# Three down-projections of a two-block layer: every second slab's remainder by ScalarE and an adding transfer

## The chip, the cores and the metric

The program runs on one core of a Trainium2 chip. A core has five engines that work beside each other, each with its own queue of instructions, and they meet through semaphores: TensorE (PE) multiplies, VectorE (DVE) and ScalarE (ACT) work element by element, GpSimd (POOL) does so too and its queue also issues transfers, and SyncE (SP) here only issues transfers. Sixteen DMA engines carry out the transfers of all queues. The metric is the time of one execution in device microseconds. A number like L487 is a line of the kernel before.

## The reference, cut to what matters

Two residual blocks work on 256 tokens of width 2048, in float32. The first has three attention branches, the second a pooling and a convolution branch and, at its end, a feed-forward part of width 8192. The change touches only that last part:

```
u = rms_norm(h, g_pre_mlp)
f = jnp.square(jax.nn.relu(u @ w_up)) @ w_down      # w_up 2048 x 8192, w_down 8192 x 2048
h = h + rms_norm(f, g_post_mlp)
```

## The kernel before

**Products in three passes.** TensorE multiplies in the rounded type fp32r. To keep the precision of float32 each weight w is split into `high`, w rounded to fp32r, and a remainder `low = w - high`; the left operand x is split in the same way. Each product then runs as x_high * high, x_high * low and x_low * high into the same bank (L607 to L609).

**Slabs.** All weights of the program form one stream of slabs of 512 KB. A slab of a down-projection is two blocks of 128 rows by 512 columns, and takes 12 matmuls on TensorE (two blocks, two tiles of tokens, three passes). Four stations handle each slab n:
1. SP loads it into `stage_rows`, which has STAGES = 8 slots, when slab n-8 has been split (`load_slab`, L464).
2. ScalarE rounds it into `high_rows`, which has PAIRS = 4 slots, as `low_rows` has, when TensorE is done with slab n-4 (`round_high`, L476). The count of finished slabs is the semaphore `used`.
3. VectorE writes the remainder into `low_rows` (`subtract_low`, L487) and raises `split_done`.
4. TensorE waits for `split_done` and multiplies (`multiply`).

**Order.** Each engine's order is fixed in the program. ScalarE and VectorE split the slab that is four ahead of the one just finished, and between slabs they do the other work of the stage (`stream`). The feed-forward part runs in four quarters of the hidden width: `w_up0` to `w_up3`, each followed by its `w_down0` to `w_down3`. A `w_down` job has 4 steps of 512 output columns with 8 slabs each, so 32 slabs. Its left operand `f_pair` was made in the `w_up` job before it. After each step VectorE adds the two banks of results to `y_rows`. In this stage ScalarE has nothing but the rounding.

**The POOL queue** issues a few transfers over the whole program: the bias rows for the gates (L757), the table `toep` (L720), a second copy of x (L772), and two gain vectors, each spread to 128 partitions, well ahead of the feed-forward part (L795, L796). In the last job it scales six pieces of the output (L802).

Of the kernel before, what the change touches and what calls it, by code (L numbers as in the profile page):

```python
# [23 lines left out]
F32R = mybir.dt.float32r  # L24
# [141 lines left out]
def build(nc, A, out):  # L166
    ctx = ExitStack()
    with ctx:
# [127 lines left out]
        def s(name):  # L296
            if name not in S:
                S[name] = sem(name)
            return S[name]
# [152 lines left out]
        stream_of_slabs = [(job, step, idx) for _, job in order for step in range(job.steps) for idx in range(job.S)]  # L452


        def load_slab(sp, job, i, u, idx):
            step = i * job.unroll + u
            n, n_static = job.slab(i, u, idx)
            p, _, k, kt, _ = job.pieces[idx]
            slot = n_static % STAGES
            sp.wait_ge(split_done, n + 1)  # L460
            sp.sem_inc(issued, 1)
            rows = slice((p.row0 + k) * P, (p.row0 + k + kt) * P)
            src = p.w[rows, bass.ds(p.col0 + step * p.stride, p.cols)] if p.stride else p.w[POOL_ORDER[step], :, :]
            sp.dma_start((stage_rows if p.by_rows else stage)[:, slot, 0:kt, 0:p.cols], src.rearrange("(k p) n -> p k n", p=P)).then_inc(landed[slot], 16)  # L464

        def round_high(act, job, i, u, idx):
            n, n_static = job.slab(i, u, idx)
            p, _, k, kt, _ = job.pieces[idx]
            slot, pr = n_static % STAGES, n_static % PAIRS
            act.wait_ge(landed[slot], 16 * (n_static // STAGES + 1) + i * (16 * (job.unroll * job.S // STAGES)))  # L470
            if job is jobs["w_up_first"] and idx < 3:
                act.activation(first_high[:, idx], stage_rows[:, slot], ACT.Copy).then_inc(high_done, 1)
                return
            act.wait_ge(used, n + 1)
            src, high = (stage_rows, high_rows) if p.by_rows else (stage, w_high)
            act.activation(high[:, pr, 0:kt, 0:p.cols], src[:, slot, 0:kt, 0:p.cols], ACT.Copy).then_inc(high_done, 1)  # L476

        def subtract_low(dve, job, i, u, idx):
            n, n_static = job.slab(i, u, idx)
            p, _, k, kt, _ = job.pieces[idx]  # L480
            slot, pr = n_static % STAGES, n_static % PAIRS
            dve.wait_ge(high_done, n + 1)
            if job is jobs["w_up_first"] and idx < 3:
                dve.tensor_tensor(first_low[:, idx], stage_rows[:, slot], first_high[:, idx].bitcast(F32), ALU.subtract).then_inc(split_done, 1)
                return
            src, high, low = (stage_rows, high_rows, low_rows) if p.by_rows else (stage, w_high, w_low)
            dve.tensor_tensor(low[:, pr, 0:kt, 0:p.cols], src[:, slot, 0:kt, 0:p.cols],  # L487
                              high[:, pr, 0:kt, 0:p.cols].bitcast(F32), ALU.subtract).then_inc(split_done, 1)
# [89 lines left out]
        def multiply(pe, job, i, u, beside=None, between=None, first_slab=None):  # L578
            for idx, (p, part, k0, kt, last) in enumerate(job.pieces):
# [16 lines left out]
                    pe.wait_ge(s(name), before + ((0 if p.stride else 2 * u) + k0 + kt + 1) // 2)  # L596
                if not by_k:
                    pe.wait_ge(split_done, STAGES + n + 1)
                for k in range(kt if p.rows else 0):
                    if by_k:  # L600
                        by_k(idx, k)
                    first, final = k0 + k == 0, last and k == kt - 1
                    high, low = (v[:, pr, k, 0:p.cols] for v in ((high_rows, low_rows) if p.by_rows else (w_high, w_low)))
                    for t in range(2):
                        bk = acc[:, 2 * bank + t, 0:p.cols]
                        x_high, x_low = (p.rows[:, k0 + k, half, t * P:(t + 1) * P] for half in range(2))
                        pe.matmul(bk, x_high, high, start=first, stop=False)  # L607
                        pe.matmul(bk, x_high, low, start=False, stop=False)  # L608
                        mm = pe.matmul(bk, x_low, high, start=False, stop=final)  # L609
# [43 lines left out]
        def _(sp):  # L653

            def other_params():
                sp.dma_start(params[:, N0:PARAMS], A["params"][:, N0:PARAMS]).then_inc(s("params_in"), 16)
                sp.dma_start(relT[:], A["rel_bias_t"]).then_inc(s("params_in"), 16)
                sp.dma_start(sinks, A["sinks_b"].partition_broadcast(P)).then_inc(s("sinks_in"), 16)

            x_of_rows = A["x"][0] if A["x"].shape[0] == 1 else A["x"]  # L660
            for name in names:
                job = jobs[name]
                if name == "mem_kv":
# [19 lines left out]
                            other_params()  # L683
                    sp.wait_ge(s("pair_ready"), 8)
                    sp.dma_start(mem_in[:], A["mem"].rearrange("(t p) d -> p t d", p=P)).then_inc(s("mem_rows_in"), 16)
                    continue
                repeat(sp, job.steps, job.unroll, lambda i, u: [load_slab(sp, job, i, u, idx) for idx in range(job.S)])
            for e in range(8):
# [7 lines left out]
        def _(pool):  # L696
# [70 lines left out]
                load_bias(n)  # L767

            pool.wait_ge(s("pv_copied"), len(HEADS))
            pool.dma_start(meta_in[:], A["meta_2"]).then_inc(s("meta_in"), 16)  # L770
            pool.dma_start(meta_t[:], A["meta_t"]).then_inc(s("meta_in"), 16)
            pool.dma_start(x_rows[:], (A["x"][0] if A["x"].shape[0] == 1 else A["x"]).rearrange("(t p) d -> p t d", p=P)).then_inc(s("x_back"), 16)  # L772
            gated(5, late[:, L_BQ:L_BQ + 6, :], L_BGATE, 6)
            for n in (10, 11):
                load_bias(n)
# [16 lines left out]
                    reach *= 2  # L792
                pool.sem_inc(s("windowed"), 1)
            pool.wait_ge(used, PAIRS + jobs["conv_out"].slab0)
            pool.dma_start(mix_gain[:], A["g_post_mix_2"].partition_broadcast(P)).then_inc(s("mix_gain_in"), 16)  # L795
            pool.dma_start(gain_rows[:], A["g_post_mlp_2"].partition_broadcast(P)).then_inc(s("gain_in"), 16)  # L796
            pool.wait_ge(s("gain_in"), 16)
            for e in range(6):
                r, t = e // 2, e % 2
                v = y_rows[:, t, r * ROW:(r + 1) * ROW]  # L800
# [5 lines left out]
        def _(act):  # L806
# [72 lines left out]
            def beside_mem(n):  # L879
                if n == 6:  # L880
                    act.wait_ge(s("x_in"), 64)
                    row_squares(x_in, "x", 0, "input_squared")
                if n == 7:
                    act.wait_ge(s("input_squared"), 1)
                    row_squares(x_in, "x", 1, "input_squared")
                    chain_root(0)
                if n == 10:
                    act.wait_ge(s("params_in"), 32)
                if n == 14:
                    mem_evacuate(0, mk_rows)  # L890
                if 11 <= n < 15:
                    for q in (2 * (n - 11), 2 * (n - 11) + 1):
                        high_unit(hT, "norm_g", q, 8)
                if n == 15:
                    mem_evacuate(1, mv_rows)
# [220 lines left out]
            def beside_up_b(n):  # L1116
                silu("w_up_b", 5, 16, L_BGATE, 3, n)
                merged_high("w_up_b", n)
                if n == 34:
                    act.wait_ge(s("meta_in"), 32)  # L1120
                    act.wait_ge(s("sums_set"), 1)
                    for r in range(4):
                        if r >= 1:
                            act.wait_ge(s("meta_squared"), r)
                        act.activation(rstd[0:META, 0:ROW], meta_in[:, r * ROW:(r + 1) * ROW], ACT.Square,
                                       accum_out=sums_1[0:META, 2, r:r + 1]).then_inc(s("meta_squared"), 1)
# [216 lines left out]
        def _(pe):  # L1343
# [332 lines left out]
            products("w_up_first", lambda n: turn_h2(3) if n == 4 else None, turn_rest)  # L1676
            for q in range(4):
                products(f"w_up{q}", turn_f if q == 0 else None)
                products(f"w_down{q}", (lambda n: None) if q == 3 else None)


        @block.vector
        def _(dve):
# [105 lines left out]
            def beside_mem(n):  # L1789
# [4 lines left out]
                    for t in range(2):  # L1794
                        dve.tensor_scalar(x_in[:, t, :], x_in[:, t, :], rs_col("x", t), None, ALU.mult).then_inc(s("x_scaled"), 1)
                if n == 9:
                    dve.wait_ge(s("params_in"), 32)
                    for i, (a, b) in enumerate((("q_norm_a", "k_norm_a"), ("q_norm_c", "k_norm_c"), ("q_norm_b", "k_norm_b"))):
                        link(dve.tensor_tensor(k_gain[:, i:i + 1], column(a), column(b), ALU.mult))
                if n == 12:  # L1800
# [47 lines left out]
            def head_logits(h):  # L1848
# [24 lines left out]
                dve.wait_ge(dve_link, link.n)  # L1873
                if kind == "B":
                    if c == 0:
                        dve.wait_ge(s("sinks_in"), 16)
                    link(dve.tensor_scalar(negmax[:, b, :], negmax[:, b, :], sinks[:, c:c + 1], -1.0, ALU.max, ALU.mult))
                elif kind == "C":
                    by_token = rs[:, RS["cq"] + c:RS["cq"] + c + C_HEADS + 1:C_HEADS]
# [220 lines left out]
            def wo_body(i, u, part):  # L2100
# [1 line left out]
                r = 2 * i + u  # L2102
                cols = slice(r * ROW, (r + 1) * ROW)
                if r == 0:
                    dve.wait_ge(s("x_back"), 16)
                for t in range(2):
                    dve.tensor_tensor(h_rows[:, t, cols], banks[:, t, :], x_rows[:, t, cols], ALU.add).then_inc(s("h1_rows"), 1)
                dve.wait_ge(s("h1_rows"), 2 * r + 2)
# [8 lines left out]
            def beside_wo(n):  # L2117
                merged_low("w_o", n)
                if n == META_AT + 1:
                    dve.wait_ge(s("meta_in"), 32)  # L2120
                    dve.wait_ge(s("merged_ready"), 8)
                    dve.wait_ge(s("meta_squared"), 4)
                    g0 = COL["g_pre_mix_2"]
# [205 lines left out]
            def mixed_body(i, u, part):  # L2329
# [2 lines left out]
                    return  # L2332
                banks, _ = group_done(dve, jobs["w_o_2"], i, u)
                if r == 0:
                    dve.wait_ge(s("mix_gain_in"), 16)
                for t in range(2):
                    dve.wait_ge(s("mix_squared"), 2 * r + t + 1)
                    gained(banks, r, t)
# [109 lines left out]

            def last_down():

                dve.wait_ge(s("gain_in"), 16)
                dve.wait_ge(s("row_squared"), 6)
                link(dve.tensor_reduce(out_rest, row_sums[:, :, 0:3], AX, ALU.add))
                link(dve.scalar_tensor_tensor(out=out_rest, in0=out_rest, scalar=1.0 / D, in1=eps_3, op0=ALU.mult, op1=ALU.add))
# [70 lines left out]
```

## Time and profile before

| | |
|---|---|
| two runs | 2048.28 and 2049.4 us, median 2048.84 us |
| span of the profiled execution | 2046.3 us |
| its own time | not listed apart from the two runs; they lie 2.0 to 3.1 us above the span |
| TensorE busy | 2034.2 us, 99% |
| VectorE, ScalarE, GpSimd busy | 66%, 46%, 4% |
| granted TensorE clock, mean | 0.999 of full speed |
| DMA | 389.23 MB, mean 190 GB/s |

The span runs from the first to the last instruction. Busy time says how long an engine had work under way, not whether somebody waited for it. The ends of matmuls are modelled, and a matmul of 512 columns is shown with 0.39 us although the next one starts 0.227 us after it; the time of a slab is therefore read from the starts. A transfer's time to landing runs from its issue to the moment at which its semaphore is complete.

### The profile page before, as it was taken

Reading aid. Unit: us, or ns where it says so; the run is one execution under the profiler, and the core shown is the slowest. Engines: PE = TensorE matmul, PEld = TensorE weight load, DVE = VectorE, ACT = ScalarE, POOL = GpSimd, SP = SyncE. Lnnn points to the kernel's source line nnn. Section 1 sums busy time; section 2 is a strip of 40 time slices with the busy share of each in tenths; the row PEclk is TensorE's granted clock in tenths of the full one; section 3 lists DMA queues with packets and bytes.
Section 4 is the critical chain, followed back from the end, with each engine's and each line's share of the span. In section 5 each row is a group of like instructions: output and inputs, shape, how many; then the busy total and the mean of one; then the engine's idle time right before and its main releaser. Section 6 shows DMA issues by size and latency. Waiting matters only on the chain.

```text
span 2046.3 us, 29256 instructions
## 1 busy us (share of the span) xinstructions
PE 2034.2 (99%) x10572; PEld 1732.4 (85%) x10572; DVE 1358.7 (66%) x1815; ACT 948.2 (46%) x1225; POOL 80.7 (4%) x91
## 2 busy tenths in 40 slices
PE   9999999999999999999999999999999999999998
PEld 7888898888888888999888888888888888888886
DVE  6766756576756565678999756576556556645655
ACT  6645444565544444433444644553333333333343
POOL 0000102001011000002000000000000000000001
PEclk9999999999999999999999999999999999999999
DMA  9687555555566555555666565655565565555652
GB/s 348 196 199 189 176 155 182 183 168 180 185 217 220 192 188 187 171 175 158 193 194 200 181 232 185 196 171 189 194 189 185 194 195 181 196 191 184 194 195 103
DMA packets 265468, 389.23 MB, mean 190 GB/s; under 512 B 12504, under 2 KB 147032, under 8 KB 264571
## 3 DMA queue, kind: packets, MB, share of 16 engines
q1 hardware_dynamic: 262587, 377.19, 57.7%
q0 software_dynamic: 2624, 10.54, 2.0%
q8 instruction: 69, 1.13, 0.2%
q14 instruction: 44, 0.36, 0.1%
q10 hardware_dynamic: 144, 0.01, 0.0%
HBM read 385.02 MB, written 2.54 MB: 189 GB/s over the span
## 4 chain that ended last, share of the span: by engine, by line
PE 98%; SPq 1%; DMA 1%; DVE 0%; ACT 0%; issue 0%; DVEq 0%
PE acc L607 19%; PE acc L609 19%; PE acc L608 19%; PE acc L630 18%; PE acc L628 10%; PE acc L622 2%; PE acc L620 2%; PE acc L621 2%; PE acc L626 1%; PE aux L1489 1%; PE aux L1573 1%; DMA stage_rows<-in_w_mem_kv 1%; PE aux L1503 0%; PE acc L546 0%; PE acc L545 0%; PE acc L544 0%
## 5 line engine op out<-in xcount | busy, mean ns | idle before, releaser
L487 DVE TENSOR_TENSOR low_rows<-stage_rows,high_rows 128x1024 fp32r<-128x1024 f32 x438 | 540.2, 1237 | 404.1 <-ACT high_rows L476 399.2
L476 ACT ACTIVATE high_rows<-stage_rows 128x1024 fp32r<-128x1024 f32 x438 | 462.3, 1059 | 581.7 <-PE acc L609 531.0
L487 DVE TENSOR_TENSOR w_low<-stage,w_high 128x1024 fp32r<-128x1024 f32 (+1 forms) x264 | 320.7, 1221 | 230.8 <-ACT w_high L476 226.3
L476 ACT ACTIVATE w_high<-stage 128x1024 fp32r<-128x1024 f32 (+1 forms) x264 | 276.2, 1047 | 417.0 <-PE acc L630 298.9
L630 PE MATMUL acc<-u,w_high 128*128 128x512 f32 x900 | 247.9, 394 | 0.0
L607 PE MATMUL acc<-high_rows,f_pair 128*128 128x512 f32 x496 | 193.0, 389 | 0.0
L608 PE MATMUL acc<-low_rows,f_pair 128*128 128x512 f32 x496 | 192.9, 389 | 0.0
L609 PE MATMUL acc<-high_rows,f_pair 128*128 128x512 f32 x496 | 192.9, 389 | 0.0
L630 PE MATMUL acc<-hT,w_high 128*128 128x512 f32 x645 | 177.5, 394 | 0.0
L630 PEld LDWEIGHTS acc<-u,w_high 128*128 128x128 f32 x900 | 152.9, 189 | 19.0
L628 PEld LDWEIGHTS acc<-u,w_low 128*128 128x128 f32 x960 | 146.8, 188 | 20.6
L628 PE MATMUL acc<-u,w_low 128*128 128x256 f32 x960 | 152.5, 281 | 0.0
L607 PE MATMUL acc<-high_rows,hT 128*128 128x512 f32 x384 | 151.8, 395 | 0.0
L609 PE MATMUL acc<-high_rows,hT 128*128 128x512 f32 x384 | 149.6, 390 | 0.0
L608 PE MATMUL acc<-low_rows,hT 128*128 128x512 f32 x384 | 149.6, 390 | 0.0
L630 PEld LDWEIGHTS acc<-hT,w_high 128*128 128x128 f32 x645 | 109.6, 189 | 13.4
L628 PEld LDWEIGHTS acc<-hT,w_low 128*128 128x128 f32 x688 | 104.0, 189 | 15.6 <-issue 2.7
L628 PE MATMUL acc<-hT,w_low 128*128 128x256 f32 x688 | 112.0, 285 | 0.0
L620 PE MATMUL acc<-uT,w_high 128*128 128x272 f32 x384 | 111.1, 289 | 0.0
L622 PE MATMUL acc<-uT,w_high 128*128 128x272 f32 x384 | 110.8, 288 | 0.0
L621 PE MATMUL acc<-uT,w_low 128*128 128x272 f32 x384 | 110.4, 288 | 0.0
L608 PEld LDWEIGHTS acc<-low_rows,f_pair 128*128 128x128 f32 x496 | 93.1, 188 | 19.4
(409 smaller groups left out, 3348.0 us busy)
## 6 DMA issues: line engine op xcount, KB each, us to landing
stage_rows<-in_w_in SPq DMA_DIRECT2D x160, 512.0 KB, 3.6
stage<-in_w_in SPq DMA_DIRECT2D x136, 512.0 KB, 3.5
stage_rows<-in_w_down SPq DMA_DIRECT2D x128, 512.0 KB, 4.3
stage<-in_w_up SPq DMA_DIRECT2D x120, 512.0 KB, 3.9
stage_rows<-in_w_o SPq DMA_DIRECT2D x64, 512.0 KB, 3.6
stage_rows<-in_w_pool_out SPq DMA_DIRECT2D x16, 512.0 KB, 3.8
stage_rows<-in_w_conv_out SPq DMA_DIRECT2D x16, 512.0 KB, 4.5
stage_rows<-in_w_mem_kv SPq DMA_DIRECT2D x14, 512.0 KB, 11.6
```

The lines of the kernel that those rows point to most:

```text
L476: act.activation(high[:, pr, 0:kt, 0:p.cols], src[:, slot, 0:kt, 0:p.cols], ACT.Copy).then_inc(high_done, 1)
L487: dve.tensor_tensor(low[:, pr, 0:kt, 0:p.cols], src[:, slot, 0:kt, 0:p.cols], high[:, pr, 0:kt, 0:p.cols].bitcast(F32), ALU.subtract).then ...
L607: pe.matmul(bk, x_high, high, start=first, stop=False)
L608: pe.matmul(bk, x_high, low, start=False, stop=False)
L609: mm = pe.matmul(bk, x_low, high, start=False, stop=final)
L620: pe.matmul(dst, tile(w_high, k), b, start=first, stop=False)
L621: pe.matmul(dst, tile(w_low, k), a, start=False, stop=False)
L622: mm = pe.matmul(dst, tile(w_high, k), a, start=False, stop=final)
L626: pe.matmul(bk, tile(w_high, 0), p.rhs(0)[0], start=True, stop=False, skip_group_check=True)
L628: pe.matmul(bk[:, 0:T], tile(w_low, k), p.rhs(k0 + k)[1], start=False, stop=False, skip_group_check=True)
L630: mm = pe.matmul(bk, tile(w_high, k), p.rhs(k0 + k)[0], start=False, stop=last and k == kt - 1, skip_group_check=True)
L1489: mm = pe.matmul(aux[:, logits_bank(h), lo:hi], q[:, t * P:(t + 1) * P], k[:, 0:hi - lo], start=True, stop=True)
```

## The change

In `w_down0`, `w_down1` and `w_down2`, in the first three of the four steps, the slabs with an odd index (1, 3, 5, 7) get their remainder in another way. That is 3 x 3 x 4 = 36 slabs of the 128 of the down-projections.
- ScalarE rounds such a slab as before, and then writes the slab once more, rounded and negated, into its slot of `low_rows`. Negated and rounded it is -high.
- GpSimd's queue then issues a transfer that reads the same weights from device memory again and adds them to that slot: w + (-high) = low. Two semaphores in turn, `low_added0` and `low_added1`, say that it has landed.
- VectorE leaves the subtraction out. It waits for the one before and raises `split_done`.
- TensorE waits, ahead of an added slab, for its transfer too. SP waits for the transfer of slab n-8 before it loads slab n into the same slot of `stage_rows`, which ScalarE has read by then.
- SP's and TensorE's loops over these jobs are written out step by step.
- Waits are merged: the sinks count with the parameters, the two meta transfers with the second copy of x, and the two gains with each other.

```diff
@@ -452,12 +452,27 @@
         stream_of_slabs = [(job, step, idx) for _, job in order for step in range(job.steps) for idx in range(job.S)]
 
 
+        ADDED = {}
+        for q in range(3):
+            job = jobs[f"w_down{q}"]
+            for step in range(job.steps - 1):
+                for idx in range(1, job.S, 2):
+                    ADDED[job.slab0 + step * job.S + idx] = len(ADDED)
+        low_added = [sem(f"low_added{b}") for b in range(2)]
+
+        def wait_added(eng, n):
+
+            e = ADDED.get(n) if isinstance(n, int) else None
+            if e is not None:
+                eng.wait_ge(low_added[e % 2], 16 * (e // 2 + 1))
+
         def load_slab(sp, job, i, u, idx):
             step = i * job.unroll + u
             n, n_static = job.slab(i, u, idx)
             p, _, k, kt, _ = job.pieces[idx]
             slot = n_static % STAGES
             sp.wait_ge(split_done, n + 1)
+            wait_added(sp, n - STAGES if isinstance(n, int) else None)
             sp.sem_inc(issued, 1)
             rows = slice((p.row0 + k) * P, (p.row0 + k + kt) * P)
             src = p.w[rows, bass.ds(p.col0 + step * p.stride, p.cols)] if p.stride else p.w[POOL_ORDER[step], :, :]
@@ -474,6 +489,8 @@
             act.wait_ge(used, n + 1)
             src, high = (stage_rows, high_rows) if p.by_rows else (stage, w_high)
             act.activation(high[:, pr, 0:kt, 0:p.cols], src[:, slot, 0:kt, 0:p.cols], ACT.Copy).then_inc(high_done, 1)
+            if isinstance(n, int) and n in ADDED:
+                act.activation(low_rows[:, pr], stage_rows[:, slot], ACT.Copy, scale=-1.0).then_inc(s("low_negated"), 1)
 
         def subtract_low(dve, job, i, u, idx):
             n, n_static = job.slab(i, u, idx)
@@ -482,6 +499,10 @@
             dve.wait_ge(high_done, n + 1)
             if job is jobs["w_up_first"] and idx < 3:
                 dve.tensor_tensor(first_low[:, idx], stage_rows[:, slot], first_high[:, idx].bitcast(F32), ALU.subtract).then_inc(split_done, 1)
+                return
+            if isinstance(n, int) and n in ADDED:
+                dve.wait_ge(split_done, STAGES + n)
+                dve.sem_inc(split_done, 1)
                 return
             src, high, low = (stage_rows, high_rows, low_rows) if p.by_rows else (stage, w_high, w_low)
             dve.tensor_tensor(low[:, pr, 0:kt, 0:p.cols], src[:, slot, 0:kt, 0:p.cols],
@@ -596,6 +617,7 @@
                     pe.wait_ge(s(name), before + ((0 if p.stride else 2 * u) + k0 + kt + 1) // 2)
                 if not by_k:
                     pe.wait_ge(split_done, STAGES + n + 1)
+                    wait_added(pe, n)
                 for k in range(kt if p.rows else 0):
                     if by_k:
                         by_k(idx, k)
-                sp.dma_start(sinks, A["sinks_b"].partition_broadcast(P)).then_inc(s("sinks_in"), 16)
+                sp.dma_start(sinks, A["sinks_b"].partition_broadcast(P)).then_inc(s("params_in"), 16)
 
...
@@ -684,6 +706,11 @@
                     sp.wait_ge(s("pair_ready"), 8)
                     sp.dma_start(mem_in[:], A["mem"].rearrange("(t p) d -> p t d", p=P)).then_inc(s("mem_rows_in"), 16)
                     continue
+                if name in ("w_down0", "w_down1", "w_down2"):
+                    for step in range(job.steps):
+                        for idx in range(job.S):
+                            load_slab(sp, job, step // job.unroll, step % job.unroll, idx)
+                    continue
                 repeat(sp, job.steps, job.unroll, lambda i, u: [load_slab(sp, job, i, u, idx) for idx in range(job.S)])
             for e in range(8):
                 t, r = e // 4, e % 4
@@ -767,9 +794,9 @@
                 load_bias(n)
 
             pool.wait_ge(s("pv_copied"), len(HEADS))
-            pool.dma_start(meta_in[:], A["meta_2"]).then_inc(s("meta_in"), 16)
-            pool.dma_start(meta_t[:], A["meta_t"]).then_inc(s("meta_in"), 16)
-            pool.dma_start(x_rows[:], (A["x"][0] if A["x"].shape[0] == 1 else A["x"]).rearrange("(t p) d -> p t d", p=P)).then_inc(s("x_back"), 16)
+            pool.dma_start(meta_in[:], A["meta_2"]).then_inc(s("rows_back"), 16)
+            pool.dma_start(meta_t[:], A["meta_t"]).then_inc(s("rows_back"), 16)
+            pool.dma_start(x_rows[:], (A["x"][0] if A["x"].shape[0] == 1 else A["x"]).rearrange("(t p) d -> p t d", p=P)).then_inc(s("rows_back"), 16)
             gated(5, late[:, L_BQ:L_BQ + 6, :], L_BGATE, 6)
             for n in (10, 11):
                 load_bias(n)
@@ -792,9 +819,15 @@
                     reach *= 2
                 pool.sem_inc(s("windowed"), 1)
             pool.wait_ge(used, PAIRS + jobs["conv_out"].slab0)
-            pool.dma_start(mix_gain[:], A["g_post_mix_2"].partition_broadcast(P)).then_inc(s("mix_gain_in"), 16)
-            pool.dma_start(gain_rows[:], A["g_post_mlp_2"].partition_broadcast(P)).then_inc(s("gain_in"), 16)
-            pool.wait_ge(s("gain_in"), 16)
+            pool.dma_start(mix_gain[:], A["g_post_mix_2"].partition_broadcast(P)).then_inc(s("gains_in"), 16)
+            pool.dma_start(gain_rows[:], A["g_post_mlp_2"].partition_broadcast(P)).then_inc(s("gains_in"), 16)
+            pool.wait_ge(s("gains_in"), 32)
+            for n, e in ADDED.items():
+                job, step, idx = stream_of_slabs[n]
+                p, _, k, kt, _ = job.pieces[idx]
+                rows = p.w[(p.row0 + k) * P:(p.row0 + k + kt) * P, step * ROW:(step + 1) * ROW]
+                pool.wait_ge(s("low_negated"), e + 1)
+                pool.dma_start(low_rows[:, n % PAIRS], rows.rearrange("(k p) n -> p k n", p=P).bitcast(F32R), accum_op=ALU.add).then_inc(low_added[e % 2], 16)
             for e in range(6):
@@ -1676,7 +1709,7 @@
             products("w_up_first", lambda n: turn_h2(3) if n == 4 else None, turn_rest)
             for q in range(4):
                 products(f"w_up{q}", turn_f if q == 0 else None)
-                products(f"w_down{q}", (lambda n: None) if q == 3 else None)
+                products(f"w_down{q}", lambda n: None)
 
 
         @block.vector
```

The remaining hunks only put the merged semaphores into the waits: `params_in` at 48, `rows_back` at 48, `gains_in` at 32.

ScalarE's order, from the last slab of `w_up0` to slab index 3 of `w_down0`; `w_high` and `high_rows` are the rounded slabs, `landed` says that a load is there. Before:

```order
L476 ACTIVATE w_high<-stage 128x1024 [waits used,landed2]
L476 ACTIVATE high_rows<-stage_rows 128x1024 [waits used,landed3]
L476 ACTIVATE high_rows<-stage_rows 128x1024 [waits used,landed4]
L476 ACTIVATE high_rows<-stage_rows 128x1024 [waits used,landed5]
L476 ACTIVATE high_rows<-stage_rows 128x1024 [waits used,landed6]
L476 ACTIVATE high_rows<-stage_rows 128x1024 [waits used,landed7]
```

and with the change:

```order
L491 ACTIVATE w_high<-stage 128x1024 [waits used,landed2]
L491 ACTIVATE high_rows<-stage_rows 128x1024 [waits used,landed3]
L491 ACTIVATE high_rows<-stage_rows 128x1024 [waits used,landed4]
L493 ACTIVATE low_rows<-stage_rows 128x1024
L491 ACTIVATE high_rows<-stage_rows 128x1024 [waits used,landed5]
L491 ACTIVATE high_rows<-stage_rows 128x1024 [waits used,landed6]
L493 ACTIVATE low_rows<-stage_rows 128x1024
L491 ACTIVATE high_rows<-stage_rows 128x1024 [waits used,landed7]
```

After the rounding of every odd slab stands the negated one, and the roundings of later slabs are queued behind it.

SP's queue at the start of `w_down0`, before, where the loop's registers stand between the loads:

```order
L117 ISA
L464 ISA [waits split_done]
L464 DMA stage_rows<-in_w_down 128x2x512
L460 REGISTER_ALU
L464 ISA [waits split_done]
L464 DMA stage_rows<-in_w_down 128x2x512
```

and with the change:

```order
L117 COMPARE_AND_BRANCH
L479 DMA stage_rows<-in_w_down 128x2x512 [waits split_done] x9
L479 DMA stage_rows<-in_w_down 128x2x512 [waits split_done,low_added0]
L479 DMA stage_rows<-in_w_down 128x2x512 [waits split_done]
L479 DMA stage_rows<-in_w_down 128x2x512 [waits split_done,low_added1]
L479 DMA stage_rows<-in_w_down 128x2x512 [waits split_done]
```

The first nine loads wait as before. From then on every second load also waits for an adding transfer, and the loads behind it wait with it.

## Rows read from the trace of the kernel before

**Rows 1.** The page, part 1: busy us, share, instructions of each engine.
```profile
PE 2034.2 (99%) x10572; PEld 1732.4 (85%) x10572; DVE 1358.7 (66%) x1815; ACT 948.2 (46%) x1225; POOL 80.7 (4%) x91
```
**Rows 2.** Windows of the first and third down-projection: busy us and instructions of each engine.
```profile
core 0: us, PE busy (x) PEld busy (x) DVE busy (x) ACT busy (x) POOL busy (x), PEclk, DMA share, GB/s
1421.00:1508.00 87.00, 87.00 (x386) 72.02 (x385) 45.62 (x42) 33.93 (x32) 0.00 (x0) 1.00 0.59 193
...
1770.00:1857.00 87.00, 87.00 (x391) 72.24 (x390) 45.65 (x43) 33.72 (x33) 0.00 (x0) 1.00 0.58 193
```
**Rows 3.** Waits of TensorE's weight loads, 1340 to 2041 us: us, times, longest.
```profile
PEld aux L1573 <- DVE tmp L2405: 0.5, 1, 0.5
```
**Rows 4.** Timeline of weight loads, first down-projection: start us, us, engine, line, operation.
```profile
1439.70 0.19 PEld L607 LDWEIGHTS acc<-high_rows,f_pair 128*128 128x128 f32 x1
...
1447.86 0.19 PEld L607 LDWEIGHTS acc<-high_rows,f_pair 128*128 128x128 f32 x1
```
**Rows 5.** Timeline of ScalarE, there and one pair before.
```profile
1346.44 2.02 ACT L476 ACTIVATE w_high<-stage 128x1024 fp32r<-128x1024 f32 x2
...
1440.19 1.06 ACT L476 ACTIVATE high_rows<-stage_rows 128x1024 fp32r<-128x1024 f32 x1 [1.66 <-PE acc L609]
1442.91 1.06 ACT L476 ACTIVATE high_rows<-stage_rows 128x1024 fp32r<-128x1024 f32 x1 [1.66 <-PE acc L609]
```
**Rows 6.** Timeline of VectorE, same place.
```profile
1441.28 1.23 DVE L487 TENSOR_TENSOR low_rows<-stage_rows,high_rows 128x1024 fp32r<-128x1024 f32 x1 [1.49 <-ACT high_rows L476]
1444.00 1.23 DVE L487 TENSOR_TENSOR low_rows<-stage_rows,high_rows 128x1024 fp32r<-128x1024 f32 x1 [1.50 <-ACT high_rows L476]
```
**Rows 7.** DMA issues of all: queue, count, KB each, median us to landing.
```profile
stage_rows<-in_w_down SPq DMA_DIRECT2D x128, 512.0 KB, 4.3
...
stage_rows<-in_w_mem_kv SPq DMA_DIRECT2D x14, 512.0 KB, 11.6
...
bias_ring<-in_gate_bias POOLq DMA_DIRECT2D x12, 256.0 KB, 4.0
toep<-bias_rows POOLq DMA_DIRECT2D x8, 288.0 KB, 9.1
...
x_rows<-in_x POOLq DMA_DIRECT2D x1, 2048.0 KB, 11.8
...
mix_gain<-in_g_post_mix POOLq DMA_DIRECT2D x1, 1024.0 KB, 7.7
gain_rows<-in_g_post_mlp POOLq DMA_DIRECT2D x1, 1024.0 KB, 10.3
...
small<-in_sinks_b SPq DMA_DIRECT2D x1, 6.0 KB, 10.8
```
**Rows 8.** The POOL queue's issues at line 757: ns min/median/max.
```profile
L757 POOL DMA_DIRECT2D bias_ring<-in_gate_bias x12: 538/538/572, 351.4 to 661.2; - x12
```
**Rows 9.** Windows: the start, and a 2 MB transfer of the POOL queue.
```profile
0.00:100.00 100.00, 95.86 (x494) 80.42 (x495) 67.57 (x117) 64.30 (x107) 1.72 (x11) 1.00 0.82 275
14.00:32.00 18.00, 18.00 (x81) 14.89 (x80) 11.74 (x18) 10.49 (x17) 0.00 (x0) 1.00 1.05 386
606.00:616.00 10.00, 10.00 (x46) 8.28 (x45) 7.83 (x8) 4.52 (x6) 5.39 (x3) 1.00 0.99 353
```
**Rows 10.** Timeline of the POOL queue: two issues.
```profile
604.81 0.72 POOL L772 DMA_DIRECT2D x_rows<-in_x  x1
...
1193.84 0.55 POOL L796 DMA_DIRECT2D gain_rows<-in_g_post_mlp  x1
```
**Rows 11.** Sources of four lines: ns min/median/max, first and last start us.
```profile
L658 SPq DMA_DIRECT2D small<-in_sinks_b x1: 552/552/552, 21.1 to 21.1; - x1
L1799 DVE TENSOR_TENSOR k_gain<-params x3: 151/160/160, 44.2 to 44.6; 128x1 f32<-128x1 f32 x3
L1125 ACT ACTIVATE rstd<-meta_in x4: 615/630/632, 703.8 to 706.0; 16x512 f32<-16x512 f32 x4
L2327 DVE TENSOR_TENSOR mixed<-acc,mix_gain x8: 681/684/685, 1264.2 to 1332.2; 128x512 f32<-128x512 f32 x8
```

More of the change, by code:

```diff
@@ L887, in beside_mem @@
                 if n == 10:
-                    act.wait_ge(s("params_in"), 32)
+                    act.wait_ge(s("params_in"), 48)
                 if n == 14:
@@ L1119, in beside_up_b @@
                 if n == 34:
-                    act.wait_ge(s("meta_in"), 32)
+                    act.wait_ge(s("rows_back"), 48)
                     act.wait_ge(s("sums_set"), 1)
@@ L1796, in beside_mem @@
                 if n == 9:
-                    dve.wait_ge(s("params_in"), 32)
+                    dve.wait_ge(s("params_in"), 48)
                     for i, (a, b) in enumerate((("q_norm_a", "k_norm_a"), ("q_norm_c", "k_norm_c"), ("q_norm_b", "k_norm_b"))):
@@ L1875, in head_logits @@
                     if c == 0:
-                        dve.wait_ge(s("sinks_in"), 16)
+                        dve.wait_ge(s("params_in"), 48)
                     link(dve.tensor_scalar(negmax[:, b, :], negmax[:, b, :], sinks[:, c:c + 1], -1.0, ALU.max, ALU.mult))
@@ L2104, in wo_body @@
                 if r == 0:
-                    dve.wait_ge(s("x_back"), 16)
+                    dve.wait_ge(s("rows_back"), 48)
                 for t in range(2):
@@ L2119, in beside_wo @@
                 if n == META_AT + 1:
-                    dve.wait_ge(s("meta_in"), 32)
+                    dve.wait_ge(s("rows_back"), 48)
                     dve.wait_ge(s("merged_ready"), 8)
@@ L2334, in mixed_body @@
                 if r == 0:
-                    dve.wait_ge(s("mix_gain_in"), 16)
+                    dve.wait_ge(s("gains_in"), 32)
                 for t in range(2):
@@ L2449, in last_down @@
             def last_down():
-                dve.wait_ge(s("gain_in"), 16)
+                dve.wait_ge(s("gains_in"), 32)
                 dve.wait_ge(s("row_squared"), 6)
```

## Prediction, made before the changed kernel was run

> **What bounds the kernel now.** I read the busy time by engine first: TensorE is busy 2034.2 of 2046.3 us and VectorE 66% [rows 1]. The reader is to see that VectorE, which the change relieves, has a third of its time free. Next the windows of the down-projections that the change touches, of which the first and the third stand in the rows: in each 87 us TensorE is busy for all 87.00, VectorE for 45.6, ScalarE for 33.7 to 33.9, and the DMA engines have a share of 0.58 to 0.59 at 193 GB/s [rows 2]. Then the waits of TensorE's weight loads from 1340 us to the end: one, of 0.5 us, in another place [rows 3]. So TensorE never waits for VectorE in these stages, and taking work off VectorE can give back nothing there. Even if every idle microsecond of TensorE in the whole span went away, the gain would be 2046.3 - 2034.2 = 12 us, or 0.6%.
>
> What is left to work out is whether the new way gets its remainder to TensorE in time. The timeline gives the deadline. TensorE loads the first weights of a slab at 1439.70 and of the third after it at 1447.86 [rows 4]: 8.16 us for three slabs, 2.72 us for one. The rounding of slab n starts when slab n-4 is done, at 1440.19 [rows 5], and TensorE takes up slab n with that load at 1447.86.
>
> **The change part by part.**
>
> *VectorE* loses 36 subtractions of 1.23 us [rows 6], 44 us that nobody waited for: worth 0. Its order stays. At an added slab it only waits for the subtraction before, long over, and counts the slab as split.
>
> *ScalarE* gains 36 negated roundings. Two roundings of this size back to back take 2.02 us [rows 5], so the second ends at 1440.19 + 2.02 = 1442.21. The next rounding is due at 1442.91 [rows 5], so ScalarE keeps 0.7 us spare, and its queue costs 0.
>
> *The adding transfer* is the term that decides. VectorE starts 0.03 us after ScalarE's end (1440.19 + 1.06 = 1441.25, start 1441.28 [rows 5, 6]); with such a step the POOL queue issues at about 1442.25. From there to 1447.86 are **5.6 us** in which 512 KB must be issued, read, added and landed. Before the change the remainder was ready at 1442.51 and had 5.3 us to spare; this cover is used up entirely. No transfer of the kernel adds, so its landing time L is bounded by the nearest rows. All times to landing of this queue contain its own issue of 0.54 to 0.72 us [rows 8, 10].
> - From below: plain transfers of the POOL queue land in 4.0 us at 256 KB and 7.7 us at 1024 KB [rows 7]; between them 512 KB would take 4.0 + 3.7 x 256/768 = 5.2 us. That is just in time, with stall 0.
> - The middle: an adding transfer reads 512 KB from device memory and the same 512 KB of the destination, so 1024 KB go in. The row of that size says 7.7 us.
> - From above: 288 KB in short rows of 1 KB, a count of pieces (288) close to the 256 of this transfer, take 9.1 us. Plain 512 KB transfers in full queues, at the start, take 11.6 us [rows 7].
>
> I take 7.7 us, the row with the same bytes read and with ordinary loads beside it. It comes d = 7.7 - 5.6 = 2.1 us late.
>
> How stalls add up: slab n is late by d if the three slabs ahead of it ran without a wait. A stall at n-2, which is also an added slab, moves the start of n later, but not the moment at which its own preparation began, so it counts towards n. With s(n) + s(n-2) = d for neighbours, whatever the split, 12 added slabs of a job cost 6d, and the three jobs **18d = 18 x 2.1 = 38 us**. The last eight slabs of each job, and the fourth job, go the old way.
>
> A page of the Trainium skill, Collectives: The Full Stack, in the section on the bandwidth ceiling and the fold count, says that an adding DMA needs two source reads and so runs at half the rate of a copy. No transfer in this trace shows it. If it held at the size of the 5.2 us estimate, with only its moving part doubled, the transfer would land after about 7.7 us as well.
>
> *Load on the DMA engines.* One 512 KB load per 2.72 us is the 193 GB/s of the window. An adding transfer for every second slab is 96 GB/s, or 193 if both reads count: 290 to 386 GB/s. At the start the engines moved 386 GB/s at a full share, and 353 with a 2 MB transfer of the POOL queue beside the loads [rows 9]. On the low count there is room. On the high count a pair of slabs needs 1.57 MB + 0.52 MB = 2.10 MB, which at 353 to 386 GB/s is 5.4 to 5.9 us against 5.44 us of TensorE: 0 to 0.5 us per added slab, up to 18 us. The 38 us above already stretch the pair to 6.5 us, so this bound lies inside them and is not added.
>
> *SP* must now wait, before it loads slab n, until the add of slab n-8 has landed. Loads of later slabs queue behind it. The add lands about when TensorE takes up slab n-8, and ScalarE wants the load five slabs later: 13.6 us, less 4.3 us of landing [rows 7], leaves 9 us. Cost 0. SP's and TensorE's loops over these jobs are written out. The weight loads show no wait at the loops' returns [rows 3], so this is worth 0 too.
>
> *POOL* issues 36 transfers of 0.54 us in 12 pairs of slabs per job, with nothing else in its queue until it scales the output in the fourth job. Cost 0.
>
> *Shared semaphores.* The parameters now wait for the sinks too: issued at 21.1, landed 10.8 later, at 31.9, first needed at 44.2. The meta rows wait for the 2 MB of x: 604.81 + 11.8 = 616.6, needed at 703.8. The two gains are there at 1193.84 + 10.3 = 1204.1 and needed at 1264.2, and the first adding transfer is due after 1410 [rows 7, 10, 11]. Each costs 0, and the cover is 12, 87 and 60 us.
>
> *POOL against VectorE.* Twelve issues of the POOL queue took 0.54 to 0.57 us, with VectorE about 0.6 busy, and the one of x_rows 0.72 [rows 8, 10]; at an added slab VectorE is idle until 1444.00 [rows 6]. I take no delay. If each issue had to wait out one subtraction of 1.23 us, the sum would be 18 x 1.2 = 22 us more; this is part of rival 3. The Trainium skill, SBUF — State Buffer, in its box on the trap that DVE blocks DMA, has such a rule: in VectorE's two-port modes GpSimd can't write descriptors. The 0.72 us may be a trace of it; the twelve others show none.
>
> **Sum.** The span is 2046.3 us. The two runs are 2048.28 and 2049.4, median 2048.84, so 2.5 us lie around the span. The own time of the profiled execution is not listed apart from these. 2048.8 + 38 = **2087 us**, 1.8% slower. A measurement of this kernel tells from no change about 2%, or 41 us: the limits are 2008 and 2090 us, and 2090 is reached at d = 2.3, L = 7.9 us. The forecast stands close to this edge.
>
> **The rivals.**
> 1. *In time* (chance 0.22). L is at most 5.8 us and nothing stalls: 2047 to 2053 us. For it: the 5.2 us between two measured sizes, and DMA engines that are only 0.6 busy. Against it: the second read, and not a tenth of a microsecond of slack.
> 2. *The forecast* (0.40). L is 6 to 9 us, so 18 x 0.4 to 18 x 3.4 = 7 to 61 us: 2056 to 2110 us. Somewhat over half of this, 0.22, lies below 2090.
> 3. *The adding transfer is slow piece by piece* (0.36, of which 0.04 for the issue that waits for VectorE), the case on the other side of 2%. Place: the wait of TensorE ahead of every other added slab. Price: L of 9.1 us costs 18 x 3.5 = 63 us, and 11.6 us costs 18 x 6.0 = 108, so 2112 to 2157 us. If one transfer at a time can't be done within 5.44 us of service, every added slab stalls by the excess, and it goes on from there: 8 us of service would be 36 x 2.6 = 92 us. It decides from L = 7.9 us. For it: the toep row, 9.1 us for 288 pieces. Against it: that one moves 1 KB rows into few partitions.
> 4. *VectorE was in the way after all* (0.01): folds or activations come sooner and the 12 us of idle time shrink, to 2040 us. Against it: the waits show no such place. Over 2% faster is out of reach of 12 us.
>
> A fall of TensorE's clock through the stalls I hold unlikely: TensorE was idle for 4 of the first 100 us and the granted clock was 1.00 [rows 9], and the stalls here are 2 us in 11 us.
>
> **Numbers.** Likeliest time 2087 us, the forecast's. The range is 2047 to 2150 us: from no stall to d = 5.6; above it lies about 0.12, below it 0.02. Same: 0.22 + 0.22 + 0.01 = 0.45. Slower by over 2%: 0.18 + 0.36 = 0.54. Faster by over 2%: 0.01, for what no row shows.
>
> **What would show it.** TensorE's waits get a row "high_rows or low_rows, released by a DMA" of about 18 stalls of 2 us in the three stages; each of these lasts about 100 us in place of 87. The table of DMA issues has the adding transfer 36 times, at 7.7 us. VectorE's busy time falls by 44 us, ScalarE's rises by 38. The DMA share in these stages goes from 0.59 to 0.8 or more. The fourth job and all stages ahead of 1410 us stay as they are. I am wrong if the transfer lands in under 5.6 us (no row, 2049 us), or if it lands in 7.7 us and TensorE waits at each of the 36 slabs and not at half of them; or if loads of the ordinary kind come late behind it, which would show as waits of ScalarE for stage_rows.

## The result and the profile after

The changed kernel takes 2104.25 us (two runs, 2104.22 and 2104.28) against 2048.84 us: ratio 1.0273, 95% interval 1.0256 to 1.029, so 55 us or 2.7% slower. The profiled execution took 2104.28 us with a span of 2102.4 us. The forecast was 2087 us, the range 2047 to 2150 us; the time lies in the forecast's own case (2056 to 2110 us), 17 us above the value taken, and beyond the 2% at which I had set no change apart from slower.

The page of the changed kernel, part 1 (busy us, share, instructions; compare [rows 1]) and part 6 (count, KB, median us to landing):

```profile
PE 2049.5 (97%) x10572; PEld 1737.7 (83%) x10572; DVE 1315.5 (63%) x1779; ACT 982.0 (47%) x1261; POOL 123.7 (6%) x127
...
low_rows<-in_w_down POOLq DMA_DIRECT2D x36, 512.0 KB, 6.6
```

VectorE does 43 us less, as worked out; ScalarE 34 us more, which is 36 x 0.96 us, the step in the part on ScalarE, and not the 38 us named among the signs. TensorE is idle 52.9 us in place of 12.1, and busy 15 us longer with the same 10572 matmuls. Both have to be explained.

The window that answers to [rows 2], columns as there:

```profile
1421.00:1508.00 87.00, 73.11 (x302) 58.06 (x301) 23.59 (x24) 36.86 (x37) 13.09 (x11) 0.96 0.90 227
```

TensorE got 302 matmuls done where it did 386, the granted clock is 0.96 and the DMA share rose from 0.59 to 0.90. TensorE's waits from 1410 to 1905 us (total us, times, longest), where [rows 3] had none on the weights:

```profile
PE acc L629 <- DMA low_rows<-in_w_down: 35.7, 19, 3.4
PE acc L629 <- DVE low_rows L508: 5.1, 2, 2.5
```

The second row is put down to VectorE, which had skipped the slab; the adding transfers of these two slabs landed at 1459.76 and 1661.06, and TensorE went on at 1459.89 and 1661.20, so both rows are one thing: 21 stalls, 40.8 us. The source view of the transfer (ns min/median/max of the issue; us to landing):

```profile
L830 POOL DMA_DIRECT2D low_rows<-in_w_down x36: 1179/1190/1231, 1417.4 to 1882.7; - x36
...
DMA to landing us min/median/max: 6.0/6.6/9.3
```

The issue takes 1.19 us where plain ones took 0.54 [rows 8]. The timelines of ScalarE, the POOL queue and TensorE (start us, us, engine, line, operation, idle before) at the second stall of the first job:

```profile
1427.37 1.06 ACT L491 ACTIVATE high_rows<-stage_rows 128x1024 fp32r<-128x1024 f32 x1 [3.11 <-PE acc L631]
1428.33 1.04 ACT L493 ACTIVATE low_rows<-stage_rows 128x1024 fp32r<-128x1024 f32 x1
```
```profile
1429.67 1.18 POOL L830 DMA_DIRECT2D low_rows<-in_w_down  x1 [5.68 <-ACT low_rows L493]
1435.11 1.19 POOL L830 DMA_DIRECT2D low_rows<-in_w_down  x1 [4.25 <-ACT low_rows L493]
```
```profile
1438.49 0.61 PE L629 MATMUL acc<-high_rows,f_pair 128*128 128x512 f32 x1 [3.06 <-DMA low_rows<-in_w_down]
1438.90 0.63 PE L630 MATMUL acc<-low_rows,f_pair 128*128 128x512 f32 x1
1439.33 0.63 PE L631 MATMUL acc<-high_rows,f_pair 128*128 128x512 f32 x1
...
1442.20 0.40 PE L629 MATMUL acc<-high_rows,f_pair 128*128 128x512 f32 x1
```

The transfer of 1429.67 lands at 1438.35, after 8.7 us, and TensorE goes on at 1438.49. The next one, of 1435.11, lands after 6.2 us, and its slab has no stall. That is the predicted pattern: a stall at every other added slab (in a few places of the first and third job it is two in a row). After this stall of 3 us the matmuls start 0.427 us apart and not 0.227, for nine of them: the granted clock is at its lower level (0.65 on the mean of 1440 to 1443 us), and back at the full one from 1442.20.

Summed over the starts of neighbouring matmuls in the three jobs: gaps of over 0.5 us hold 45.4 us more than the ordinary 0.227 (the 21 stalls, and four of 0.54 to 0.57 us at the lower clock with 1.3 us), intervals of 0.3 to 0.5 us (58 of them, mostly at the lower clock) 10.2 us more. Together 55.6 us, the whole loss. Of the 15 us of longer busy time 10.2 are these slower matmuls; the rest is that the page lets each matmul ahead of a stall end later than the next one would have started.

### The profile page after: what moved, and what is told of

It is laid out like the page before. It is cut to its first block, busy times and chain, and to the rows that moved or that the text cites. A ratio compares the mean times of both kernels' runs of the same rounds, so it can differ in the third digit from the quotient of the medians.

```text
span 2102.4 us, 28986 instructions
## 1 busy us (share of the span) xinstructions
PE 2049.5 (97%) x10572; PEld 1737.7 (83%) x10572; DVE 1315.5 (63%) x1779; ACT 982.0 (47%) x1261; POOL 123.7 (6%) x127
## 3 DMA queue, kind: packets, MB, share of 16 engines
q8 instruction: 74, 1.21, 0.2%
## 4 chain that ended last, share of the span: by engine, by line
PE 89%; DMA 7%; ACT 2%; SPq 1%; issue 1%; DVE 0%; DVEq 0%; ACTq 0%; POOLq 0%
PE acc L629 17%; PE acc L631 17%; PE acc L630 17%; PE acc L652 17%; PE acc L650 9%; DMA low_rows<-in_w_down 6%; PE acc L644 2%; PE acc L642 2%; PE acc L643 2%; PE acc L648 1%; ACT high_rows L491 1%; ACT low_rows L493 1%; PE aux L1522 1%; PE aux L1606 1%; DMA stage_rows<-in_w_mem_kv 0%
## 5 line engine op out<-in xcount | busy, mean ns | idle before, releaser
L508 DVE TENSOR_TENSOR low_rows<-stage_rows,high_rows 128x1024 fp32r<-128x1024 f32 x402 | 496.2, 1238 | 484.6 <-ACT high_rows L491 480.1
L629 PE MATMUL acc<-high_rows,f_pair 128*128 128x512 f32 x496 | 199.6, 402 | 40.7 <-DMA low_rows<-in_w_down 35.7
L631 PE MATMUL acc<-high_rows,f_pair 128*128 128x512 f32 x496 | 196.9, 397 | 0.0
L629 PEld LDWEIGHTS acc<-high_rows,f_pair 128*128 128x128 f32 x496 | 95.7, 193 | 68.6 <-issue 49.0
L631 PEld LDWEIGHTS acc<-high_rows,f_pair 128*128 128x128 f32 x496 | 95.6, 193 | 20.9
L642 PE MATMUL acc<-uT,w_high 128*128 128x272 f32 x384 | 111.1, 289 | 0.0
```

The source lines that it names most:

```text
L642: pe.matmul(dst, tile(w_high, k), b, start=first, stop=False)
```

## The experiments

Times are medians; ratios are to runs of the kernel before on the same chip, 2048.4 us for experiments 1, 3, 4 and 5 and 2048.0 us for 2, 6, 7 and 8. Each trace is of one execution.

**1. The rest of the edit alone.**

```diff
-                for idx in range(1, job.S, 2):
+                for idx in ():
```

> The loops over the three jobs are written out and the semaphores merged as in the change, but no slab is added: VectorE subtracts for all of them. My theory, that all of the loss comes from the adding transfers: within 3 us of the kernel before (2049). Rival, that the written-out loops (more instructions to fetch) or the merged waits cost something: 2055 us or more, with waits of TensorE outside the added slabs.

Measured: 2047.63 us, ratio 0.9997 (0.9987 to 1.0007), and no wait of TensorE in the three jobs. The written-out loops and the merged semaphores cost nothing that shows (the interval ends at 0.07%, 1.4 us).

**2. No transfer.** The POOL loop is left out, and what waited for the transfers waits for the negated rounding.

> The POOL queue issues none of the 36 transfers; TensorE and SP wait for the negated rounding alone. The weights are not added to it, so the remainder is wrong. All theories that put the loss on the transfers: 2046 to 2050 us, though ScalarE does 36 operations more. Rival, that ScalarE's second operation delays the rounding behind it: 2052 us or more, with waits of VectorE and TensorE for high_rows.

Measured: 2047.45 us, ratio 0.9996 (0.9987 to 1.0006), no wait of TensorE. ScalarE's 36 operations cost nothing that shows. With experiment 1, all of the 55 us hang on the transfers, and the relief of VectorE brings nothing.

**3. A plain transfer in the place of the adding one.**

```diff
-  ..., accum_op=ALU.add).then_inc(low_added[e % 2], 16)
+  ...).then_inc(low_added[e % 2], 16)
```

> The 36 transfers of the POOL queue are plain ones: they overwrite the slot with the weights instead of adding to it, so the remainder is wrong (it is the weight). Same bytes from device memory, same waits. If the second read of the adding transfer is what makes it late: it lands in 5.2 to 6.2 us, TensorE waits 0 to 0.8 us at every other added slab, 2049 to 2064 us. Rival, that the queue, its issue of 1.19 us or the loads beside it set the time: landing stays at 6.6 us in the median and 8 us for the late ones, 2095 us or more.

The remainder is then wrong, and only the time counts. Measured: 2070.96 us (four runs, 2066.87 to 2077.19), ratio 1.0113 (1.009 to 1.0136): 23 us above the kernel before, between the two expectations. The issue and the landing of the plain transfer, then TensorE's waits in the three jobs:

```profile
L830 POOL DMA_DIRECT2D low_rows<-in_w_down x36: 696/705/715, 1417.8 to 1854.3; - x36
...
DMA to landing us min/median/max: 4.0/5.8/8.0
```
```profile
PE acc L629 <- DMA low_rows<-in_w_down: 16.1, 15, 1.8
```

The adding is thus worth 33 of the 55 us, and 23 us are lost with a plain transfer of the same shape in its place. Its longer issue (1.19 against 0.70 us) is part of the 33: 18 x 0.49 = 9 us, an estimate by the rule of the prediction. In the same 87 us from 1421 the queues' table gives the engines' time by queue (packets, MB, share of 16 engines), first for the plain kernel, then for the changed one:

```profile
q0 software_dynamic: 3139, 6.04, 23.8%
```
```profile
q0 software_dynamic: 3187, 6.13, 42.7%
```

Per 512 KB (11.5 and 11.7 of them) that is 1.80 us of all 16 engines for a plain transfer and 3.18 us for an adding one, 1.8 times as much for the same bytes. The Trainium skill, Collectives: The Full Stack, in the section on the bandwidth ceiling and the fold count, gives the add of a ReduceScatter two source reads and half the rate of a copy. The 1.8 measured here is near that factor of two, for another kind of transfer; that the second read is the reason is not shown by a run.

**4. Half as many.**

```diff
-                for idx in range(1, job.S, 2):
+                for idx in range(1, job.S, 4):
```

> Only slabs 1 and 5 of a step are added, 18 in place of 36; VectorE subtracts for the others. Latency theory: a late transfer no longer helps the next one, so all 18 slabs stall by the full d, as 18 of 36 did. With landings of 6.6 to 8 us that is 18 x 1.2 to 18 x 2.6 us, 2071 to 2096 us and up to 10 us more from the lower clock: nearly the cost of all 36. Load theory (the DMA engines are full): half the added bytes bring 240 GB/s, far from the 386 seen at the start, so the stalls all but vanish, 2049 to 2058 us.

Measured: 2064.18 us, ratio 1.0077 (1.006 to 1.0094). Its landing, and TensorE's waits in the three jobs:

```profile
DMA to landing us min/median/max: 6.0/6.2/6.8
```
```profile
PE acc L629 <- DMA low_rows<-in_w_down: 11.4, 18, 1.0
```

Now all 18 added slabs stall, where about half of 36 did: as the latency theory says, a neighbour no longer helps. But each stalls by 0.8 us only (14.3 us by the starts), since no landing takes 8 us any more. With an issue 2.30 us after the rounding's start, a landing of 6.2 us and TensorE's demand 7.67 us after that start (1447.86 - 1440.19 [rows 4, 5]), d is 2.30 + 6.2 - 7.67 = 0.8 us. So the rule holds, and L is not a fixed number of the transfer. Neither expectation had this. Beside each of these transfers fly 0.76 MB of SP's loads on the mean, but never another adding transfer; in the change neighbours overlap, mostly by 2 to 3 us.

**5. SP not held by the transfers.**

```diff
-            wait_added(sp, n - STAGES if isinstance(n, int) else None)
+            if isinstance(n, int) and n - STAGES in ADDED:
+                sp.wait_ge(s("low_negated"), ADDED[n - STAGES] + 1)
```

> SP waits, before it loads into a slot of an added slab, only for ScalarE's negated rounding and not for the transfer; all else as in the change. Bunching theory: the late transfers take 8 us and the others 6, because each landing sets free two loads of 512 KB at once, ahead of the next adding transfer. Then all transfers land in about 6.3 us, d falls from 2.4 to about 1, and the clock doesn't drop: 18 x 1 = 18 us, 2062 to 2072 us. Rival, that the adding transfers disturb each other: landings and time stay, 2100 to 2108 us.

Measured: 2105.84 us, ratio 1.0276 (1.0259 to 1.0293). The trace is of the slowest of the four runs, 2108.88 us.

```profile
DMA to landing us min/median/max: 7.1/8.4/9.4
```
```profile
PE acc L630 <- DMA low_rows<-in_w_down: 46.8, 31, 2.9
```

The bunching theory is wrong: with loads issued evenly no transfer takes 6 us, they take 7.1 to 9.4, about 8.4 in the middle. The short landings of the change go with SP being held back: beside the 20 that landed within 6.8 us SP's queue moved 0.41 MB on the mean, beside the 15 of 7.4 us and more 1.21 MB, and here 1.41 MB. Free of that, 31 slabs stall, by 1.5 us each, 52.1 us by the starts. The sum over neighbours stays what the rule asks: 18 x (2.30 + 8.36 - 7.67) = 54 us. The rival, that the adding transfers disturb each other, had the time right (2100 to 2108 us) but not the landings, and it is not excluded: here neighbours overlap by 2.8 us, and in experiment 4, where none do, 0.76 MB of loads went with only 6.2 us. How much of the 8.4 us comes from the loads and how much from the adding transfer beside it stays open.

**6. The negated rounding first.** ScalarE's two operations on an added slab change places.

> ScalarE writes the negated rounding of an added slab before the rounding, so the transfer is issued 0.96 us earlier; nothing else changes, TensorE needs the rounding only 5 us later. Latency theory (each pair of neighbouring added slabs costs d): d falls by 0.96 us, 18 x 0.96 = 17 us less and fewer falls of the clock, 2078 to 2090 us. Load theory (the DMA engines' rate sets the pace of the three stages): the time stays at 2101 to 2107 us, and the transfers land later by what they start earlier.

Measured: 2094.74 us, ratio 1.0222 (1.0205 to 1.0239), 9.5 us less than the change and not 17. The stalls hold 37.3 us by the starts, 8 less than in the change. The median landing went from 6.6 to 7.2 us: started 0.96 us earlier, the transfers take 0.5 us longer and give half of it back. Both theories had a part of it; what they meet in that time was not tested.

**7. Prepared up to four slabs ahead.**

```diff
+        ahead_low = [at(f"ahead_low{b}", kb, [P, 2, ROW], F32R) for b, kb in enumerate((Z + 32, Z + 36, Z + 80, Z + 116))]
...
+            for n2 in NEGATE_AT.get(n, ()) if isinstance(n, int) else ():
+                act.wait_ge(landed[n2 % STAGES], 16 * (n2 // STAGES + 1))
+                act.activation(ahead_low[ADDED[n2] % 4][:], stage_rows[:, n2 % STAGES], ACT.Copy, scale=-1.0).then_inc(s("low_negated"), 1)
...
+                if e >= 2:
+                    pool.wait_ge(low_added[e % 2], 16 * (e // 2))
```

The last two lines let POOL issue a transfer only when the one two before it has landed, so at most two are under way; SP's wait is that of experiment 5.

> The negated rounding goes to four slots of its own (in memory that is free in this stage) and is made up to four slabs earlier, as soon as the load is there; so each adding transfer has 8 to 18 us before TensorE wants it, not 5.4. 33 slabs are added in place of 36 (slab 1 of each job is left to VectorE), SP waits for the negation alone. Latency theory: no wait of TensorE for a transfer is left, landings of 8 to 9 us are hidden, 2047 to 2052 us. Load theory: the same bytes at TensorE's full pace ask for 290 GB/s written and 96 GB/s more read; if that is over what the engines do, TensorE waits on in the second and third step of each job, 2060 us or more.

Measured: 2047.30 us, ratio 0.9996 (0.9987 to 1.0006). TensorE has no wait left in the three jobs. The landing, and the window of the first 60 us of the first job (columns as in [rows 2]):

```profile
DMA to landing us min/median/max: 8.4/9.1/12.5
```
```profile
1421.00:1481.00 60.00, 60.00 (x266) 49.71 (x265) 19.00 (x19) 32.06 (x32) 10.68 (x9) 1.00 1.07 292
```

The transfers land later than in any other kernel (POOL waited 13 times for an earlier one, 59.6 us in all) and TensorE is busy 60 of 60 us. So it was latency, not rate. The DMA engines are full, though: share 1.07 at 292 GB/s, and loads of SP take 10.2 us here (median of 1421 to 1508) where they took 4.3. The stretch of adds is short and SP's lead covers it; how long it could go on was not tried. With 33 of 36 subtractions gone from VectorE and no stall, the time equals that of the kernel before within 0.1%: the relief of VectorE is worth nothing.

**8. TensorE kept at work ahead of the waits.**

```diff
+                    if isinstance(n, int) and n in ADDED:
+                        for _ in range(7):
+                            pe.transpose(aux[:, 0, P:2 * P], ident[:], ident[:])
                     wait_added(pe, n)
```

> As the change, but ahead of its wait for an adding transfer TensorE does seven 128-column transposes of a constant (about 1 us, results unused), in each of the 36 slabs. In the stalls they take the place of idle time; in the slabs without a stall they delay TensorE by 1 us, which by the rule s(n) + s(n-2) = d comes off the next stall. If the falls of the granted clock after the long waits cost time of their own, about 11 us of the 55, and come from the idling: the clock of the three stages goes from 0.96 back to 1.00, and the time falls to 2090 to 2098 us. Rival, that the clock's fall only lengthens matmuls that wait anyway: time 2102 to 2110 us.

Measured: 2099.52 us (four runs, 2098.05 to 2106.33), ratio 1.0259 (1.0238 to 1.0279), 4.7 us less than the change, between the two expectations; the intervals of the two ratios overlap, so the times alone don't tell the two kernels apart. The window of the first job:

```profile
1421.00:1508.00 87.00, 80.87 (x392) 66.19 (x390) 24.58 (x25) 37.47 (x37) 13.09 (x11) 1.00 0.91 227
```

The granted clock is back at 1.00. By the starts, the intervals of 0.3 to 0.5 us cost 3.6 us and not 10.2, the longer gaps (which now hold the transposes, 0.69 us at an added slab without a stall) 48.0 and not 45.4. The clock's fall thus had a price of its own, some 7 us by these two traces. The four runs of this kernel agree: three with a mean granted clock of 0.999 took 2098.05 to 2100.08 us, the one with 0.996 took 2106.33 us. The median landing rose from 6.6 to 7.0 us, which may be why the whole gain is smaller.

## Why the prediction was right, and where it was too low

- **Bound.** That TensorE sets the time and VectorE's relief is worth 0 was right (experiments 2 and 7).
- **Free parts.** ScalarE's operations, the loops and the semaphores cost 0, as forecast (experiments 1 and 2). ScalarE never waited for a load in the three jobs.
- **The place and the rule.** The loss sits at the wait ahead of the added slabs, at every other one in the main (21 stalls of 36, forecast 18), and s(n) + s(n-2) = d is what the experiments with half as many transfers and with SP not held show from two sides. In the change itself it holds slab by slab: with each transfer's own issue and landing, the stall and the one before it add up to the lateness of that slab less 0.1 to 0.3 us at all 21. Each of the three jobs took 105 to 106 us, not 100; the fourth took 87 us as before.
- **The size of d.** I took 5.6 us from issue to demand and L = 7.7, d = 2.1, 38 us. Measured are 45.4 us, d = 2.5. The issue comes 0.24 us later than I set it (1429.67 - 1427.37 = 2.30 us against 2.06), since POOL starts 0.3 us after ScalarE's end and not 0.03. The landing is not one number: 7.4 to 9.3 us for most of those that stall and about 6.2 for those between them. The 7.7 us of the 1024 KB row is the mean of the 21 that stall, but not the median of the 36, which I had given as a sign and which is 6.6. Put into the forecast's sum, 6.6 us gives 18 x 1.0 = 18 us; that the late ones fall on every other slab, where they count, was not foreseen, so the closeness of 38 to 45 us is in part luck. Of the POOL queue's issue I had 0.54 us; it took 1.19. The lower bound of 5.2 us was too low for an adding transfer (6.0 us at best) and somewhat low for a plain one (median 5.8 us, 13 of 36 under 5.2, experiment 3).
- **SP.** I wrote that its wait costs 0. It made no load late. But it held loads back beside every second transfer, and those landed in about 6.2 us. Without it (experiment 5) the sum was much the same, so the error is in the account, not in the time.
- **The step that failed: the clock.** I held a fall of the clock unlikely, by a stretch at the start with 4 us of idle at full clock [rows 9]. That idle time lay in six pieces, the first of 2.0 us at the very start and the others of at most 1.0 us. After six of the stalls, of 2.3 to 3.4 us, the clock went to its lower level for 6 to 14 matmuls. By the starts this is about 10 us, of which experiment 8 took 7 away; with the 7 us in d it makes the 17 us by which I was low.
- **The rivals.** *In time* failed. *Slow piece by piece* had the landing of the latest transfers (9.0 to 9.3 us) but not its price of 63 us or more; its other form, a stall at every added slab because one transfer takes over 5.44 us of service, does not show: with experiment 7's lead none stalled. That run also answers the bound on the DMA engines' load: at most 18 us forecast, 0 measured. *A wait of POOL's issue for VectorE* does not show: all 36 issues took 1.18 to 1.23 us.

## What to carry to other kernels

Before work is moved off an engine, look whether anybody waits for that engine; here nobody did, and the best version tried only equals the old time. When a transfer takes the place of an engine's operation, count the time from its release to its demand against its landing with the ordinary loads in flight, not alone; where that fails, give it more buffers and start it earlier before trying to make it shorter. And where a prepared-ahead pipeline misses its deadline by d, neighbours share the delay, and items set further apart each stall by their full d. Halving their number then brings something only if it makes d smaller, as it did here: 2.5 to 0.8 us, and the loss fell from 55 to 16 us.

## What the hardware showed

- An adding transfer of 512 KB in 2 KB rows takes 1.19 us to issue and 1.8 times the DMA engines' time of a plain one (3.18 against 1.80 us of all 16). It lands in 6.0 us at best, in 8.4 us (median of experiment 5) where SP's queue moved 150 GB/s beside it and the neighbouring adding transfers overlapped, and in 9.1 us with the engines full; the plain one in 4.0 to 8.0 us.
- The DMA engines at a share of 1.07 moved 292 GB/s with adds among the loads, where plain loads at the start reached 386 [rows 9].
- After six of the 21 stalls (of 2.3 to 3.4 us) TensorE's matmuls started 0.427 us apart and not 0.227, the lower of its two levels (1.2 and 2.4 GHz); among them are the five longest, of 2.9 us and more. After five others of 2.3 to 2.7 us they did not. What tells the one of 2.3 us from these stays open. The kernel with 18 stalls of up to 1.0 us kept a mean granted clock of 0.999.
